# Turned keys written with the page number innermost by VectorE, scores copied as plain rows by ScalarE

## The chip, the cores and the metric

The kernel runs on one core of a Trainium2 chip. Its engines are TensorE (PE), VectorE (DVE), ScalarE (ACT), GpSimd (POOL) and SyncE (SP), which here issues the loads. The metric is the device time of one execution in microseconds (us). Three runs of the kernel before took 1157.41, 1162.14 and 1161.44 us; their median is 1161.44 us.

## The reference

One step of a one-layer decoder trunk with two groups of tokens: a prompt of 512 tokens, and 8 samples (batches) of 8 new tokens each. The layer projects its normalised input to q, k, v and two convolution branches, runs block-sparse attention (8 heads of 64) and a convolution module side by side, projects their concatenation, and ends with a gated convolutional feed-forward network:

```python
h = _rmsnorm(x, g_pre_mix)
z = h @ w_in + b_in
q, k, v, cva, cvg = jnp.split(z, ...)
attn = moba_fn(q, k, v)
...
x = x + _rmsnorm(jnp.concatenate([attn, c], axis=-1) @ w_out, g_post_mix)
...
f = (jax.nn.silu(gate) * val) @ w_down
x = x + _rmsnorm(f, g_post_ffn)
```

The change lies in the attention of the samples. Each sample has 32 cached pages of 128 keys and values, found through a page table; a block is two pages. A query scores the mean key of each of 16 blocks, keeps the best three, and attends to the keys of these and to its own new ones:

```python
kp = pool_k[page_table[:, :npb * ppb]]
k_means = jnp.mean(kp.reshape(DB, npb, MOBA_BLOCK, H, D), axis=2)
idx, slot_ok = _select_blocks(qh, k_means, npb, k_sel)
...
out = _attend(qh, k_s, v_s, sel_mask, k_own, v_own, own_mask)
```

The kernel scores all 4096 cached keys, takes block sums and maxima from the scores, and masks the blocks that were not chosen.

## The kernel before

**Stages.** First x is normalised and turned, and q and the samples' k and v are projected (to about 70 us). Then follow eight sample steps, one for each sample b (about 81 to 503 us). Into them PE's other work is interleaved: steps 0 to 3 each compute a tile of the gated convolution input (`glu_tiles`), steps 4 to 7 a tile of the prompt's k and v (`kv_tiles`). Meanwhile POOL runs three of the four tiles of the 31-tap convolution, and VectorE a part of the fourth (`taps`, in steps 4 to 6). After that come the prompt's attention, the output projection and the feed-forward network (about 505 us to the end), which the change does not touch.

**One sample step.** A sample's 32 pages come in eight groups u of four pages; a page is 256 KB for keys and as much for values. SyncE loads group u of the keys into slot u % 4 of `kN` (128 keys on the partitions, page i, 512 columns of heads), as four transfers. VectorE's `turn_k` then turns 32x32 blocks of a whole group into `kT`, with one STREAM_TRANSPOSE of 2048 elements per partition; there are 8 such instructions a sample, 64 in all. PE multiplies two groups at once with the spread queries (`scores`, j = 0 to 3), into a PSUM bank of 512 columns: group, head half, and 128 columns of that group, in the order that `kT` has them. ScalarE copies the bank to `S` (`put_scores`, 32 copies in all). There the 128 columns are in the order (k i): key number k outer, page number i of four inner. `softmax` on VectorE reduces pairs of pages with that order, and `weigh` on PE picks page i of the turned probabilities.

**What sets the order.** Every engine works through its own list, written by hand, with semaphores between them. VectorE's list for step b is: `softmax(b)`, then `turn_k(b + 1, 0)` and `(b + 1, 1)`, `row_sums(b)` (L1285), `turn_k` of groups 2 and 3, the glu values (steps 0 to 3) or ten taps (steps 4 to 6), `turn_k` of groups 4 to 7, and `norm_out(b)`. Groups 4 to 7 of sample 0 are turned before the loop, groups 0 to 3 of it between the q tiles. PE's list puts `scores(b + 1, (0, 1))` between the first and second half of the values of b, and `scores(b + 1, (2, 3))` at the next step's start, after the output of b has been normalised and turned.

**Loads.** All key and value loads go through SyncE's one list (L313 keys, L323 values), in the order: values 0 to 3 of sample b, keys 0 to 5 of b + 1, values 4 to 7 of b, keys 6 and 7 of b + 1. A transfer waits until its slot is free, and with it all that stand behind it: keys of group u + 4 wait for `turn_k` of group u (`kt_ready`), and values of group u + 4 wait until `weigh` has used group u (`pv_done`), which comes after `row_sums`.

Of the kernel before, what the change touches and what calls it, by code (L numbers as in the profile page):

```python
# [22 lines left out]
ACT = mybir.ActivationFunctionType  # L23
# [67 lines left out]
def build_layer(nc, a):  # L91
    ctx = ExitStack()
    with ctx:
        def sem(name):
            return ctx.enter_context(nc.semaphore(name))
# [26 lines left out]
        def at(mem, off, *dims):  # L122
            n = 1
            for d in dims:
                n *= d
            v = mem[:, off:off + n]
            if len(dims) == 2:
                return v.rearrange("p (a b) -> p a b", a=dims[0])
            if len(dims) == 3:
                return v.rearrange("p (a b c) -> p a b c", a=dims[0], b=dims[1])  # L130
            if len(dims) == 4:
                return v.rearrange("p (a b c d) -> p a b c d", a=dims[0], b=dims[1], c=dims[2])
            return v
# [27 lines left out]
        kT = at(B, 8192, 4, 2 * H, P)  # L161
        vN = at(B, 16384, 4, 4, DA)
        wz = at(B, 24576, KC, 2, P)
        S = at(B, 26624, SUPER, 2, P)
# [85 lines left out]
        SC = [banks["sc0"], banks["sc1"]]  # L250
# [29 lines left out]
        s = {n: sem(n) for n in names}  # L280
# [562 lines left out]
        def _(act):  # L843
# [47 lines left out]
            def put_scores(b, js):  # L891
                if js[0] == 0:
                    act.wait_ge(s["p_turned"], b * 4 + START)
                for j in js:
                    act.wait_ge(s["scores_done"], b * 4 + (j + 1))
                    act.activation(S[:, 2 * j:2 * j + 2].rearrange("p a g (k i) -> p (a g) i k", i=4),  # L896
                                   SC[j % 2][:, :].rearrange("p (c i k) -> p c i k", c=4, i=4), ACT.Copy).then_inc(s["s_put"], 1)

            def exps(b):
                for g in range(2):  # L900
# [49 lines left out]

            act.wait_ge(s["vs_done"], 1)
            put_scores(0, (0, 1))
            with act.Fori(0, 4) as i:
                put_scores(i, (2, 3))
                glu_exps(i)
                exps(i)
                put_turned(i)
                spread_q(i + 1)
                put_scores(i + 1, (0, 1))
                put_out(i)  # L960
# [216 lines left out]
        def _(dve):  # L1177
# [19 lines left out]
            def turn_k(b, u, first=False):  # L1197
                dve.wait_ge(kn_full[u % 4], b * 128 + 64 * (u // 4 + 1))
                if u % 2 == 0 and not first:

                    dve.wait_ge(s["scores_done"], b * 4 + max(u // 2 - 1, 0))
                dve.transpose(kT[:, u % 4, :, :].rearrange("p c (i k) -> p i c k", i=4),  # L1202
                              kN[:, u % 4, :, :].rearrange("p i (c k) -> p i c k", k=32)).then_inc(s["kt_ready"], 1)


# [1 line left out]
            for hp in range(HP):  # L1207
                dve.wait_ge(s["zq_done"], 2 * hp + 2)
                for e in range(2):
                    dve.tensor_scalar(qZ[64 * e:64 * e + 64, hp, e, HALF:TP_], Z[1][64 * e:64 * e + 64, 0:TP_ - HALF],  # L1210
                                      b_in[64 * e:64 * e + 64, hp:hp + 1], None, ALU.add)
                dve.tensor_scalar(qTs[:, hp, :], Z[1][:, TP_ - HALF:HALF], b_in[:, hp:hp + 1], None,
                                  ALU.add).then_inc(s["zq_putV"], 1)
                turn_k(0, hp, True)
# [98 lines left out]
            def step(b, last=False, between=None):  # L1313
                softmax(b)
                if not last:
                    turn_k(b + 1, 0)
                    turn_k(b + 1, 1)
                row_sums(b)
                if not last:
                    turn_k(b + 1, 2)  # L1320
                    turn_k(b + 1, 3)
                if between:
                    between()
                if not last:
                    for u in range(4, 8):
                        turn_k(b + 1, u)
                norm_out(b)
# [373 lines left out]
```

## Time and profile before

| what | value |
|---|---|
| median of three runs | 1161.44 us |
| the profiled execution's own time | 1158.29 us |
| its span in the trace | 1156.5 us |
| mean granted TensorE clock | 0.914 of full speed |
| busy: PE, DVE, ACT, POOL | 970.9, 650.9, 372.0, 584.5 us |
| turning keys on VectorE (L1202) | 64 instructions, 144.7 us busy |
| copies of scores on ScalarE (L896) | 32 instructions, 36.5 us busy |
| start of the sample steps 0 to 7 | 81, 131, 187, 241, 299, 357, 415, 469 us |

The busy times are shares of the whole span, over stages with different limits; the change touches only the stretch up to about 500 us. The start of a sample step is the first block reduction (L1243) of its softmax. PE and PEld overlap, and a busy PE is not a PE at its peak.

### The profile page before, as it was taken

What the parts mean: (1) busy time and instruction counts of PE and PEld (TensorE: products, weight loads), DVE (VectorE), ACT (ScalarE), POOL (GpSimd) and SP (SyncE); (2) the same over time, 40 slices, a digit from 0 to 9 for tenths busy, and PEclk for the clock granted to TensorE, in tenths of its full rate; (3) what the DMA queues carried; (4) which work ended last, traced back from release to release, by engine and by line L of the source; (5) the groups of instructions that cost most, each with busy time, mean ns of one, the idle gap of its engine ahead of it and who ended that gap; (6) DMA issues with size and microseconds to landing.
All of it is one profiled execution on the core that took longest, in us unless ns stands there. A gap on an engine that the chain in (4) does not pass through costs nothing.

```text
span 1156.5 us, 21529 instructions
## 1 busy us (share of the span) xinstructions
PE 970.9 (84%) x7656; PEld 742.5 (64%) x7656; DVE 650.9 (56%) x1009; ACT 372.0 (32%) x683; POOL 584.5 (51%) x534
## 2 busy tenths in 40 slices
PE   4988676776767676778899989999999997999995
PEld 3856464545343534355464449999999997777773
DVE  3478595867798988625712335545554557423114
ACT  3123131313130313234432224433443442134223
POOL 2002999999999994003301115565555563133443
PEclk9999696979787778899899998999999999999998
DMA  9787999999989899971043002223322320222232
GB/s 319 279 277 256 318 319 317 335 323 308 322 287 324 289 317 335 313 239 43 1 164 102 8 1 73 74 73 90 91 73 73 105 77 1 91 73 73 73 87 82
DMA packets 150949, 202.40 MB, mean 175 GB/s; under 512 B 9985, under 2 KB 71426, under 8 KB 150864
## 3 DMA queue, kind: packets, MB, share of 16 engines
q1 hardware_dynamic: 149078, 197.68, 52.4%
q10 hardware_dynamic: 1828, 4.17, 1.1%
q8 instruction: 24, 0.39, 0.1%
q14 instruction: 19, 0.16, 0.0%
HBM read 196.49 MB, written 5.68 MB: 175 GB/s over the span
## 4 chain that ended last, share of the span: by engine, by line
PE 61%; SPq 14%; DVE 9%; issue 6%; DMA 5%; ACT 3%; ACTq 1%; POOL 0%; POOLq 0%; DVEq 0%
SPq L323 10%; PE tp L765 6%; PE z L765 6%; PE sc L765 6%; PE z L812 5%; PE z L741 4%; DMA B<-in_cache_k 3%; PE ob L765 3%; PE sm L765 3%; PE z L470 3%; PE sc L812 3%; PE tp L812 3%; PE sc L741 2%; SPq L313 2%; PE sc L504 2%
## 5 line engine op out<-in xcount | busy, mean ns | idle before, releaser
L1560 POOL TENSOR_SCALAR A<-A,consts 128x512 f32<-128x512 f32 x93 | 150.5, 1618 | 110.9 <-DVE A L1308 101.8
L1202 DVE STREAM_TRANSPOSE B<-B 128x2048 f32<-128x2048 f32 x64 | 144.7, 2291 | 48.1 <-DMA B<-in_cache_k 46.9
L1581 POOL TENSOR_TENSOR wulo<-B,wuhi 128x2048 fp32r<-128x2048 f32 x22 | 108.6, 4938 | 91.5 <-ACT wuhi L1070 64.5
L1563 POOL TENSOR_TENSOR A<-A 128x576 f32<-128x576 f32 x90 | 128.9, 1432 | 7.5
L556 PE MATMUL ob<-B 128*32 128x128 f32 x2048 | 81.9, 321 | 45.2 <-DMA B<-in_cache_v 44.2
L1624 POOL TENSOR_TENSOR wdlo<-B,wdhi 128x1024 fp32r<-128x1024 f32 x22 | 60.0, 2730 | 97.9 <-ACT wdhi L1137 97.9
L556 PEld LDWEIGHTS ob<-B 128*32 128x32 f32 x2048 | 67.7, 147 | 58.5 <-DMA B<-in_cache_v 55.1
L1453 DVE TENSOR_TENSOR fTlo<-A,fThi 128x1152 fp32r<-128x1152 f32 x22 | 32.0, 1455 | 105.6 <-ACT fThi L1136 101.4
L1465 DVE TENSOR_SCALAR B<-B,small 128x512 f32<-128x512 f32 x44 | 25.3, 575 | 115.9 <-ACT B L1108 115.9
L504 PE MATMUL sc<-B,A 128*32 128x256 f32 x1024 | 73.6, 449 | 4.5 <-DVE B L1202 3.9
L1468 DVE SCALAR_TENSOR_TENSOR B<-B,small 128x512 f32<-128x512 f32 x88 | 66.2, 752 | 3.1
L576 PE MATMUL z<-hT,B 128*128 128x288 f32 x256 | 63.1, 408 | 0.0
L504 PEld LDWEIGHTS sc<-B,A 128*32 128x32 f32 x1024 | 37.0, 129 | 37.4 <-issue 23.7
L896 ACT ACTIVATE B<-sc 128x512 f32<-128x512 f32 x32 | 36.5, 1141 | 76.1 <-PE sc L504 76.1
L1611 POOL COPY A<-B 128x2 f32 (+1 forms) x44 | 13.3, 302 | 94.1 <-ACT B L1108 94.1
L1136 ACT ACTIVATE fThi<-A 128x1152 fp32r (+1 forms) x22 | 25.6, 1166 | 103.8 <-PE tp L812 43.9
L576 PEld LDWEIGHTS z<-hT,B 128*128 128x128 f32 x256 | 48.3, 190 | 13.4
L765 PE MATMUL tp<-h2hi,wuhi 128*128 128x288 f32 x176 | 53.4, 303 | 2.2 <-POOL h2lo L1591 2.2
L765 PE MATMUL tp<-h2lo,wuhi 128*128 128x288 f32 x176 | 53.1, 302 | 0.0
L765 PE MATMUL tp<-h2hi,wulo 128*128 128x288 f32 x176 | 53.1, 302 | 0.0
L765 PE MATMUL z<-h2hi,wuhi 128*128 128x288 f32 x176 | 52.2, 296 | 0.0
L765 PE MATMUL sc<-h2lo,wuhi 128*128 128x288 f32 x176 | 52.0, 295 | 0.0
(317 smaller groups left out, 2558.0 us busy)
## 6 DMA issues: line engine op xcount, KB each, us to landing
B<-in_cache_k SPq DMA_DIRECT2D x256, 256.0 KB, 4.8
B<-in_cache_v SPq DMA_DIRECT2D x256, 256.0 KB, 3.9
B<-in_w_up SPq DMA_DIRECT2D x44, 512.0 KB, 4.9
B<-in_w_down SPq DMA_DIRECT2D x22, 512.0 KB, 3.7
B<-in_w_in SPq DMA_DIRECT2D x16, 512.0 KB, 7.2
B<-in_w_in SPq DMA_DIRECT2D x3, 2048.0 KB, 16.7
B<-in_w_out SPq DMA_DIRECT2D x1, 4096.0 KB, 13.9
B<-in_x_prompt SPq DMA_DIRECT2D x4, 512.0 KB, 8.9
```

The source lines that it names most:

```text
L323: sp.dma_start(home[i:P:4, v % 4, :, :], cv[bass.ds(numbers[4 * (v - u) + i], 1)].rearrange("a (g r) n -> (a r) g n", g=4)).then_inc(full[ ...
L504: ins = pe.matmul(SC[j % 2][32 * h4:32 * h4 + 32, :] .rearrange("p (a g k) -> p a g k", a=2, g=2)[:, :, g, :], qS[:, hc, :], kT[:, 2 * (j ...
L556: ins = pe.matmul(OB[32 * hp:32 * hp + 32, 0:P], w, home[:, u % 4, i, hp * P:(hp + 1) * P], start=False, stop=(u == SUPER - 1 and i == 3))
L576: ins = pe.matmul(Z[half][:, 0:HALF], wz[:, k, u, :], hT[:, k, half * HALF:(half + 1) * HALF], start=(k == 0), stop=(k == KC - 1))
L741: ins = pe.matmul(sb_[2 * (t % 2) + nh][0:m, :], mixT[:, k, t * P:t * P + m], wo[:, k, nh * TP_:(nh + 1) * TP_], start=(k == 0), stop=(k = ...
L765: ins = pe.matmul(bank8[4 * slot + n][:, 0:HALF], w[:, u * P:(u + 1) * P], x[:, k, half * HALF:(half + 1) * HALF], start=(k == 0 and j == ...
L812: ins = pe.matmul(db[nh][t][0:m, :], x[:, slot, k2, t * P:t * P + m], w[:, slot, k2, :], start=(first and k2 == 0 and j == 0), stop=(last ...
L1202: dve.transpose(kT[:, u % 4, :, :].rearrange("p c (i k) -> p i c k", i=4), kN[:, u % 4, :, :].rearrange("p i (c k) -> p i c k", k=32)).the ...
L1468: dve.scalar_tensor_tensor(dst[:, 0:TP_], src[:, j:j + TP_], w[:, j:j + 1], dst[:, 0:TP_], ALU.mult, ALU.add)
L1560: pool.tensor_scalar(dst[:, 0:TP_], glu[:, i, j:j + TP_], w, b2, *bias)
L1563: ins = pool.tensor_tensor(conv[:, i, :], conv[:, i, :], prod, ALU.add)
L1581: pool.tensor_tensor(wulo[:, slot, :, :], wu[slot].rearrange("p k u n -> p k (u n)"), wuhi[slot][:, :, :].bitcast(F32), ALU.subtract).then ...
```

## The change

Two access patterns change; no instruction is added, removed or moved on any engine, and the shapes stay (128x2048 for the turning, 128x512 for the copy). VectorE now writes `kT` with page i innermost: the 32 elements of a turned row land 4 elements (16 bytes) apart, where they lay side by side before. PE's result therefore already has the order (k i), and ScalarE's copy writes 512 elements side by side, where it wrote them 16 bytes apart before. `S` holds the same values at the same places as before.

```diff
@@ put_scores, ScalarE
-                    act.activation(S[:, 2 * j:2 * j + 2].rearrange("p a g (k i) -> p (a g) i k", i=4),
-                                   SC[j % 2][:, :].rearrange("p (c i k) -> p c i k", c=4, i=4), ACT.Copy).then_inc(s["s_put"], 1)
+                    act.activation(S[:, 2 * j:2 * j + 2].rearrange("p a g k -> p (a g k)"), SC[j % 2][:, :], ACT.Copy).then_inc(s["s_put"], 1)
@@ turn_k, VectorE
-                dve.transpose(kT[:, u % 4, :, :].rearrange("p c (i k) -> p i c k", i=4),
+                dve.transpose(kT[:, u % 4, :, :].rearrange("p c (k i) -> p i c k", i=4),
                               kN[:, u % 4, :, :].rearrange("p i (c k) -> p i c k", k=32)).then_inc(s["kt_ready"], 1)
```

## Rows read from the trace of the kernel before

**Rows 1.** Busy time in sample steps 0, 1, 4, 5, 6; PEclk, DMA share, GB/s last.
```profile
80.94:131.02 50.08, 34.98 (x478) 26.85 (x478) 35.94 (x49) 12.46 (x24) 21.03 (x20) 0.84 0.85 280
131.02:186.90 55.88, 39.84 (x511) 29.70 (x511) 41.47 (x49) 14.51 (x26) 53.05 (x47) 0.81 0.95 318
...
298.83:357.20 58.37, 39.19 (x483) 24.07 (x475) 51.84 (x64) 13.91 (x24) 55.54 (x48) 0.79 0.92 301
357.20:415.02 57.82, 40.09 (x484) 24.81 (x484) 52.01 (x63) 14.06 (x25) 55.01 (x48) 0.77 0.91 307
415.02:469.21 54.19, 37.52 (x483) 22.55 (x483) 44.28 (x64) 13.90 (x25) 29.85 (x25) 0.81 0.98 329
```

**Rows 2.** Instruction groups: the turning of keys, and what ended VectorE's idle before it.
```profile
L1202 DVE STREAM_TRANSPOSE B<-B 128x2048 f32<-128x2048 f32 x64 | 144.7, 2291 | 48.1 <-DMA B<-in_cache_k 46.9
...
  DMA B<-in_cache_k: 46.9, 13
```

**Rows 3.** Instruction groups: ScalarE's copies, written apart (L896, L884) and side by side.
```profile
L896 ACT ACTIVATE B<-sc 128x512 f32<-128x512 f32 x32 | 36.5, 1141 | 76.1 <-PE sc L504 76.1
...
L913 ACT ACTIVATE B<-tp 128x512 f32<-128x512 f32 x32 | 17.7, 593 | 12.7 <-PE tp L527 12.7
...
L884 ACT ACTIVATE A<-A 32x128 f32 x28 | 12.6, 448 | 0.2
...
L921 ACT ACTIVATE A<-tp 128x128 f32 x7 | 1.9, 277 | 140.1 <-PE tp L564 140.1
```

**Rows 4.** Instruction groups: VectorE's smallest turning, 32 elements.
```profile
L1248 DVE STREAM_TRANSPOSE small<-small 128x32 f32<-128x32 f32 x16 | 3.4, 212 | 0.6
```

**Rows 5.** VectorE in time, sample step 1: start, duration, instruction, idle before and releaser.
```profile
138.14 0.69 DVE L1243 TENSOR_REDUCE small<-B 128x8 f32<-128x512 f32 x1 [0.39 <-ACT B L896]
...
152.28 4.49 DVE L1202 STREAM_TRANSPOSE B<-B 128x2048 f32<-128x2048 f32 x2
156.69 1.05 DVE L1285 TENSOR_TENSOR small<-small 128x2 f32<-128x2 f32 x1
157.67 4.49 DVE L1202 STREAM_TRANSPOSE B<-B 128x2048 f32<-128x2048 f32 x2
162.54 3.75 DVE L1298 RECIPROCAL A<-A 128x576 f32<-128x576 f32 x1
...
167.55 4.50 DVE L1202 STREAM_TRANSPOSE B<-B 128x2048 f32<-128x2048 f32 x2
181.20 2.31 DVE L1202 STREAM_TRANSPOSE B<-B 128x2048 f32<-128x2048 f32 x1 [9.15 <-DMA B<-in_cache_k]
184.10 2.31 DVE L1202 STREAM_TRANSPOSE B<-B 128x2048 f32<-128x2048 f32 x1 [0.59 <-DMA B<-in_cache_k]
186.34 0.13 DVE L1289 RECIPROCAL small<-ob 128x1 f32<-128x1 f32 x1
```

**Rows 6.** SyncE's list and PE's first values in time, sample step 1.
```profile
141.76 17.08 SPq L313 DMA_DIRECT2D B<-in_cache_k  x24
160.45 13.23 SPq L323 DMA_DIRECT2D B<-in_cache_v  x16
174.59 4.21 SPq L313 DMA_DIRECT2D B<-in_cache_k  x8
...
158.61 5.34 PE L556 MATMUL ob<-B 128*32 128x128 f32 x128
```

**Rows 7.** VectorE in time, ahead of the sample steps and in step 0.
```profile
39.71 0.92 DVE L1210 TENSOR_SCALAR A<-z,consts 64x224 f32<-64x224 f32 x2 [4.25 <-PE z L470]
...
70.16 0.68 DVE L1230 TENSOR_TENSOR A<-tp,A 64x512 f32<-64x512 f32 x1 [4.88 <-PE tp L490]
72.13 8.89 DVE L1202 STREAM_TRANSPOSE B<-B 128x2048 f32<-128x2048 f32 x4 [1.28 <-PE sc L504]
...
125.56 2.31 DVE L1202 STREAM_TRANSPOSE B<-B 128x2048 f32<-128x2048 f32 x1 [12.48 <-DMA B<-in_cache_k]
```

## The prediction

> **What bounds the kernel now.** I read the busy times over the sample steps first, then the groups of instructions for what the two edited lines cost, and last the timelines of VectorE and of SyncE's list through one step.
>
> The busy times show two kinds of step. In step 1 the DMA engines are busy 0.95 of the time and VectorE 41.47 of 55.88 us; in steps 4 and 5 VectorE is busy 51.84 of 58.37 and 52.01 of 57.82 us, and the DMA share is 0.92 and 0.91 [rows 1]. So steps 0 to 3 go at the pace of the loads, with some room on VectorE, and steps 4 to 6, where VectorE has the ten taps as well, are close to full on it. The room has a place and a size: over all 64 turnings VectorE waits 13 times for a key load, 46.9 us in sum [rows 2]. In step 1 the reader sees it as 9.15 us ahead of group 6 and 0.59 ahead of group 7, the last but two things VectorE does in the step [rows 5]; step 0 has 12.48 us at the same place [rows 7]. Steps 2 and 3 repeat step 1.
>
> What ends a step is therefore group 7 of the next sample's keys: after it VectorE normalises the output, PE turns that and computes the next scores, and the next softmax follows. Before it stands a loop through the loads. Keys 4 and 5 wait for the turning of groups 0 and 1, values 4 to 7 stand behind them and wait for the values of the step, which wait for the row sums, and keys 6 and 7 come after those [rows 5, 6].
>
> **ScalarE's copies.** A copy of 512 columns written 16 bytes apart takes 1141 ns; the copy of the same size from PSUM written side by side takes 593 ns [rows 3]. I take 593 for the new one: 548 ns less for each of 32, 17.5 us of ScalarE in all. On the path lies little of it. Copies 0 and 1 of a sample are made while VectorE turns keys, far ahead. Copies 2 and 3 lie between the scores at the step's start and the reductions, which wait for them (0.39 us ahead of the last pair) [rows 5]; but the copy of j = 2 runs while PE computes j = 3, so a step gains one 0.55 us, 8 times: 4.4 us.
>
> **VectorE's turning.** No row shows VectorE writing single words 16 bytes apart, so the price is bounded. The one end is nothing: 2291 ns as now [rows 2]. For the other, ScalarE's rows show exactly this write pattern. From 128 columns in 277 ns and 512 in 593 follow 0.82 ns a column and 172 ns fixed when the words lie side by side; written apart, 1141 ns is (1141 - 172) / 512 = 1.89 ns a column, 1.07 more [rows 3]. If memory sets the rate and it is the same for VectorE, a turning with a fixed part of 179 ns (from 212 ns for 32 elements and 2291 for 2048, 1.03 ns an element) [rows 2, 4] takes 179 + 2048 x 1.89 = 4.05 us, 1.76 more. If the addition per word is the same, it takes 2291 + 2048 x 1.07 = 4.48 us, 2.19 more. The other copy written 16 bytes apart takes 448 ns for 128 columns against 277, 1.34 ns a column more [rows 3], which would be 2.74 us on a turning; that copy is short and covers 32 partitions, so I keep it as the far end. I take 2.0 us, between the two readings of the nearest row: a turning of 4.3 us, eight of them 34 us in a step instead of 18.
>
> The Trainium skill speaks against this change: the page Vector Engine (DVE) Microarchitecture Reference, section 5.2 Measured stream behaviour on trn2, says that a port of VectorE keeps its rate only while words come in adjacent pairs, and gives 1.71 ns a column for a destination that hops every element by 4 KiB and about 2.5 for steps of 24 words. No row here shows VectorE doing so. An estimate from that page's figures is 1.4 to 3.0 us more for a turning, and by the same sum as below a time of 1206 to 1286 us.
>
> **Where the turnings lie.** The first four, between the q tiles, are hidden: VectorE waits 4.25 us for PE after such a turning [rows 7], more than 2.0; behind the fourth the copies of q end later, but PE is busy with the values' projection until 70.13 us, as the wait of 4.88 us shows [rows 7]. Groups 4 to 7 of sample 0 run back to back for 8.89 us ahead of the first softmax [rows 7], on the path: 4 times. The other 56 stand in steps 0 to 6, in order with everything else of VectorE. So 60 x 2.0 = 120 us are added to VectorE's line.
>
> Against that stands the cover of 46.9 us. It is not free, since the loop of the loads moves too. In step 1 the turn of group 6 comes after six slower turnings, 12 us later. Its keys also land later: values 4 to 7 are let go by the values of the step, which wait for the row sums, and these come after two slower turnings, 4 us later (they were released at 156.69 + 1.05 us, and SyncE went on at 160.45) [rows 5, 6]. Of the wait of 9.15 us, 8 are used and about 1 us is left; the same in steps 2 and 3. In step 0 I reckon the loads 2 us later, so 10 of 12.48 are used. So about 4 us of waiting stays, and 43 are used up. In steps 4 to 6 the taps already fill the time, there are 5.8 us of waits among them, and the turnings cost nearly their whole 16 us a step.
>
> Who else waits: PE's scores of groups 0 and 1, 2 and 3 and the values behind them come 4 to 8 us later in the step, but have until its end. SyncE's keys 6 and 7 wait for groups 2 and 3, which are turned long before the values ahead of them are issued. After step 7 nothing is changed.
>
> **Sum.** 120 (60 turnings) - 46.9 (waits) + 4 (waits that stay) - 4.4 (copies) = 72.7 us. Against the profiled execution's 1158.3 us that is 1231 us. That execution lies 3.2 us below the median of 1161.4, and I leave it there.
>
> **The rivals.**
> 1. The waits do not give way. If late slots starve the loads so that half of the 46.9 us stays, the sum is 96 us and the time about 1254; if all of it stays, 116 us and 1274. For it: the DMA share is 0.95 in step 1, and each load stands behind a wait on VectorE [rows 1, 6]. Against it: a longer step needs no more bytes; step 1 moves 318 GB/s x 55.9 us = 17.8 MB, and over 63 us that is 283 GB/s, so the loads then have room.
> 2. VectorE writes apart at its full rate. Then only the copies count, 0.55 us a step: 1158.3 - 4.4 = 1154 us at best, no change where the loads take it up again. The place is the write side of the turning, and it decides the sign: below about 0.1 us more for a turning the kernel is no slower. For it: a turning now runs at 1.03 ns an element, as fast as any stream of VectorE in these rows [rows 2, 4], so the block is read and written at once without loss. Against it: ScalarE loses 1.07 ns a column on the same addresses [rows 3]. The same page of the Trainium skill, section 3.8 The reshape front-end and per-opcode configuration, says that the transposing block is pipelined to sustain one element per cycle and lane; if that held for any destination it would be this rival.
> 3. The price is small, 0.5 to 0.8 us, so that steps 0 to 3 hide most: 60 x 0.65 = 39, less what hides there (32 x 0.65 = 21) and 4.4, makes some 14 us and 1172. No row speaks for such a price.
>
> **How the numbers follow.** Forecast 0.73: with 1.76 us a turning 106 - 46.9 + 10 - 4.4 = 65 us, 1223; with 2.19 us 131 - 46.9 + 2 - 4.4 = 82 us, 1240; with 2.74 us 164 - 46.9 - 4.4 = 113 us, 1271. Rival 1: 0.16. Rival 2: 0.07. Rival 3: 0.04. The range from 1203 to 1274 us holds the forecast with 20 us below its lower price, and rival 1 up to its end; the rest, rivals 2 and 3 and a little above, is below 2 in 10. A difference of 0.5% (5.8 us) is about what a measurement of this kernel can tell from no change. Slower by more than that: 0.92 (forecast, rivals 1 and 3). Within: 0.05, and faster by more: 0.03, both from rival 2, whose 4.4 us lie inside the bound.
>
> **What would show it.** L1202 in the groups of the profile after: about 4.3 us if right, 2.3 if rival 2 is. L896: about 0.6 us. VectorE's waits for key loads: a few us instead of 46.9; 20 or more would be rival 1. Step 1 about 63 us long, step 4 some 73, and the stretch from the prompt's attention to the end as long as before. The prediction is wrong if the turning keeps its time, or if the steps grow by far more or less than 60 turnings less the waits.

## The result and the profile after

The changed kernel takes 1204.61 us (median of 4 runs, 1201.82 to 1206.04) against 1161.79 us of the kernel before in the same comparison: a ratio of 1.0371, 95% interval 1.0335 to 1.0407. It is slower by 43 us. The profiled executions differ by the same: 1201.82 us against 1158.29 us.

The groups of instructions of the changed kernel hold the two edited lines (the turning is L1201 now). Columns: busy time, mean ns of one, idle before with what ended it.

```profile
L1201 DVE STREAM_TRANSPOSE B<-B 128x2048 f32<-128x2048 f32 x64 | 243.9, 3907 | 12.3 <-DMA B<-in_cache_k 11.0 <-PE sc L504 1.3
...
L896 ACT ACTIVATE B<-sc 128x512 f32<-128x512 f32 x32 | 19.1, 598 | 105.6 <-PE sc L504 105.6
```

A turning takes 3907 ns where it took 2291 [rows 2]: 1616 ns more, 64 times. The copy takes 598 ns where it took 1141 [rows 3]. And the cover, the waits for key loads in which longer turnings can hide, is mostly gone: VectorE waits 11.0 us, not 46.9 [rows 2]. Each half of the change has an effect, but they are of very different weight, since a turning writes 2048 words a partition and a copy 512, and the one stands on VectorE's line and the other mostly beside it.

The busy times over the sample steps of the changed kernel (columns as in [rows 1]; PE, PEld, DVE, ACT, POOL, then PEclk, DMA share, GB/s) show where the time went. The last row is everything after the start of step 7.

```profile
86.69:140.49 53.80, 35.93 (x478) 26.77 (x478) 48.62 (x50) 10.26 (x23) 17.36 (x17) 0.82 0.72 242
140.49:198.70 58.21, 38.53 (x511) 28.01 (x511) 51.03 (x48) 12.38 (x26) 55.33 (x48) 0.82 0.93 307
...
319.22:385.63 66.41, 36.51 (x475) 21.73 (x467) 62.01 (x65) 11.39 (x24) 63.11 (x55) 0.78 0.91 302
385.63:455.10 69.47, 37.93 (x484) 22.36 (x484) 63.42 (x64) 11.70 (x25) 66.11 (x57) 0.77 0.78 261
455.10:512.58 57.48, 36.75 (x483) 22.14 (x483) 52.19 (x64) 11.67 (x25) 4.01 (x4) 0.80 0.81 268
...
512.58:1200.00 687.42, 638.67 (x3844) 511.43 (x3844) 305.74 (x565) 252.36 (x462) 257.69 (x243) 0.97 0.27 82
```

Step 1 grew by 2.3 us, step 4 by 8.0, step 5 by 11.7, step 6 by 3.3 [rows 1]. In step 5 the DMA share fell from 0.91 to 0.78 and in step 6 from 0.98 to 0.81, as the loads there now wait for VectorE: SyncE's list waits 15.8 and 13.4 us for turnings in these two steps, where it waited 2.3 and nothing. The stretch from step 7 to the end is 687.4 us, as it was (1156.5 - 469.2 = 687.3). All of the 43 us lies between 72 us and the start of step 7.

VectorE's timeline in step 1 of the changed kernel answers to [rows 5]: two slow turnings, the row sums, two more, the glu values, and then the last four, with a wait of 2.80 us where 9.15 and 0.59 stood.

```profile
158.74 7.80 DVE L1201 STREAM_TRANSPOSE B<-B 128x2048 f32<-128x2048 f32 x2
166.39 0.15 DVE L1284 TENSOR_TENSOR small<-small 128x2 f32<-128x2 f32 x1
166.42 8.04 DVE L1201 STREAM_TRANSPOSE B<-B 128x2048 f32<-128x2048 f32 x2
...
180.37 7.61 DVE L1201 STREAM_TRANSPOSE B<-B 128x2048 f32<-128x2048 f32 x2
190.78 7.47 DVE L1201 STREAM_TRANSPOSE B<-B 128x2048 f32<-128x2048 f32 x2 [2.80 <-DMA B<-in_cache_k]
```

One row in it was not expected: the row sums (L1284, before L1285) take 0.15 us where they took 1.05 [rows 5].

**The account of VectorE's line.** From the first of the four turnings ahead of the loop to the start of step 7 the kernel before needs 397.1 us (72.13 to 469.21), the changed one 440.6 us (72.02 to 512.58), 43.5 more. VectorE's busy time in that stretch rises from 316.3 to 398.9 us, of which the 60 turnings take 135.5 and 228.4: +92.9 us for the turnings, -10.4 us for all its other instructions. Its waits for key loads fall by 35.9 us, and those for the copies from 20.7 to 17.2 us, by 3.5. The sum, 92.9 - 10.4 - 35.9 - 3.5, is 43.1 us. (60 x 1.616 would be 97.0 us; in the records turnings that follow one another overlap a little, as four in a row take 14.67 us and not 15.6.)

The rows of this account, first the two stretches before and after, then the turnings and the waits for copies in them:

```profile
72.13:469.21 397.08, 276.18 (x3524) 187.58 (x3516) 316.29 (x388) 102.15 (x180) 320.85 (x276) 0.81 0.93 311
72.02:512.58 440.56, 273.40 (x3524) 183.89 (x3516) 398.87 (x388) 85.43 (x180) 320.48 (x276) 0.79 0.86 285
...
L1202 DVE STREAM_TRANSPOSE B<-B 128x2048 f32<-128x2048 f32 x60 | 135.5, 2290 | 48.1 <-DMA B<-in_cache_k 46.9 <-PE sc L504 1.3
L1201 DVE STREAM_TRANSPOSE B<-B 128x2048 f32<-128x2048 f32 x60 | 228.4, 3910 | 12.3 <-DMA B<-in_cache_k 11.0 <-PE sc L504 1.3
...
DVE small L1243 <- ACT B L896: 20.7, 12, 3.0
DVE small L1242 <- ACT B L896: 17.2, 13, 2.5
```

TensorE's granted clock in this stretch is 0.79 of full speed after and 0.81 before. That is no term of the sum: besides the waits for copies, VectorE waits for PE 1.3 us in both kernels.

### The profile page after: what moved, and what is told of

It reads as the page before. It is cut to its first block, busy times and chain, and to the rows that moved or that the text cites. A ratio compares the mean times of both kernels' runs of the same rounds, so it can differ in the third digit from the quotient of the medians.

```text
span 1200.0 us, 21529 instructions
## 1 busy us (share of the span) xinstructions
PE 968.3 (81%) x7656; PEld 738.0 (62%) x7656; DVE 740.9 (62%) x1009; ACT 354.5 (30%) x683; POOL 584.7 (49%) x534
## 4 chain that ended last, share of the span: by engine, by line
PE 59%; DVE 20%; issue 8%; SPq 6%; DMA 3%; ACT 2%; DVEq 1%; ACTq 0%; POOL 0%; POOLq 0%
DVE B L1201 10%; PE tp L765 6%; PE z L765 6%; PE sc L765 6%; PE z L812 5%; SPq L323 4%; PE z L741 3%; PE sc L504 3%; PE ob L765 3%; PE sm L765 3%; PE sc L812 3%; PE z L470 3%; PE tp L812 3%; PE sc L741 2%; DMA B<-in_cache_k 2%
## 5 line engine op out<-in xcount | busy, mean ns | idle before, releaser
L1201 DVE STREAM_TRANSPOSE B<-B 128x2048 f32<-128x2048 f32 x64 | 243.9, 3907 | 12.3 <-DMA B<-in_cache_k 11.0
L504 PE MATMUL sc<-B,A 128*32 128x256 f32 x1024 | 76.0, 456 | 17.2 <-DVE B L1201 16.6
L564 PE MATMUL tp<-consts,oN 128*128 128x128 f32 x8 | 3.6, 456 | 89.2 <-DVE oN L1291 89.2
L1570 POOL TENSOR_TENSOR A<-A,B 128x2304 f32<-128x2304 f32 x1 | 5.0, 5047 | 110.9 <-ACT B L1032 110.9
L576 PEld LDWEIGHTS z<-hT,B 128*128 128x128 f32 x256 | 48.3, 190 | 13.4
```

The lines of the kernel that those rows point to most:

```text
L504: ins = pe.matmul(SC[j % 2][32 * h4:32 * h4 + 32, :] .rearrange("p (a g k) -> p a g k", a=2, g=2)[:, :, g, :], qS[:, hc, :], kT[:, 2 * (j ...
L576: ins = pe.matmul(Z[half][:, 0:HALF], wz[:, k, u, :], hT[:, k, half * HALF:(half + 1) * HALF], start=(k == 0), stop=(k == KC - 1))
L1201: dve.transpose(kT[:, u % 4, :, :].rearrange("p c (k i) -> p i c k", i=4), kN[:, u % 4, :, :].rearrange("p i (c k) -> p i c k", k=32)).the ...
```

## The experiments

The diffs are shortened: `...` marks what is left out, `S[...]` and `SC[...]` stand for whole indices, and `kT[:, u % 4]` stands for `kT[:, u % 4, :, :]`. Where a kernel writes the turned keys or the scores in another order than the softmax expects, its results are not the reference's, but its instructions and their shapes are those of the kernel that it is compared with.

**The halves apart, and VectorE's time alone.** The first kernel takes only ScalarE's half.

```diff
-  S[:, 2*j:2*j+2].rearrange("p a g (k i) -> p (a g) i k", i=4), SC[j % 2].rearrange("p (c i k) -> p c i k", c=4, i=4)
+  S[:, 2*j:2*j+2].rearrange("p a g k -> p (a g k)"), SC[j % 2][:, :]
```

> Only ScalarE's half of the change: plain copies, turned keys side by side as before. The columns of the scores then stand in the order (i k), which the softmax takes for (k i), so keys are put to the wrong blocks; every instruction keeps its shape. Theory (VectorE's line sets the steps): copies 0.6 us, turnings 2.29 us, 0.55 us less a step, about 1157 us. Rival (the loads take the gain up in the load-bound steps 0 to 3): 1159 to 1161 us.

Measured: 1154.77 us, ratio 0.9939 (0.9921 to 0.9958) to 1161.85 us before. The copies take 597 ns, the turnings 2288. The theory was close (7 us less, 4.4 expected); the rival, that the loads take the gain up, is out, since even the upper end of the interval is 4.9 us below the time before.

The second takes only VectorE's half.

```diff
-  dve.transpose(kT[:, u % 4].rearrange("p c (i k) -> p i c k", i=4), ...)
+  dve.transpose(kT[:, u % 4].rearrange("p c (k i) -> p i c k", i=4), ...)
```

> Only VectorE's half: keys turned with the page innermost, ScalarE's copies written apart as before (so the scores are permuted once too often; shapes as before). Theory: turnings 3.9 us, and the gain of the copies gone: the changed kernel's 1204.6 us and 3.5 to 4.4 us more, about 1208 us. Rival (the copies are hidden behind the longer turnings): 1205 us as the changed kernel.

Measured: 1205.05 us, ratio 1.0374 (1.0352 to 1.0395); turnings 3910 ns, copies 1131. The group of its turning:

```profile
L1202 DVE STREAM_TRANSPOSE B<-B 128x2048 f32<-128x2048 f32 x64 | 243.8, 3910 | 12.6 <-DMA B<-in_cache_k 11.3 <-PE sc L504 1.3
```

The slow-down is in the turning alone. What the copies bring once the turnings are slow stays open: the time equals that of the full change, as the rival has it, but VectorE's waits for the copies are 21.7 us here against 17.2 with the full change, as the theory has it, and 3 to 4 us is not more than the runs of either kernel scatter.

The third kernel leaves all addresses as before and only gives VectorE more to do.

```diff
+  dve.tensor_reduce(fill[...], kN[:, u % 4].rearrange("p i n -> p (i n)")[:, 0:1408], AX.X, ALU.max)
   dve.transpose(kT[:, u % 4].rearrange("p c (i k) -> p i c k", i=4), ...)
```

> The kernel before, with a reduction of 1408 key columns (about 1.62 us, read side by side, result not used) put ahead of each of the 64 turnings on VectorE, and nothing written apart by VectorE. Theory (it is only VectorE's time): 2.29 + 1.62 = 3.91 us for each turning with its filler, so the same time as the turning-alone kernel within 3 us, about 1208 us. Rival (words written 16 bytes apart also slow others: loads into the same memory, PE's reads of the turned keys): the filler kernel is faster than the turning-alone kernel by 5 us or more.

Measured: 1207.75 us, ratio 1.040 (1.038 to 1.042). The groups of this kernel, the filler and the turning:

```profile
L1206 DVE STREAM_TRANSPOSE B<-B 128x2048 f32<-128x2048 f32 x64 | 147.0, 2297 | 0.0
L1204 DVE TENSOR_REDUCE fill<-B 128x1408 f32 x56 | 89.0, 1590 | 13.6 <-DMA B<-in_cache_k 13.6
```

1590 and 2297 ns make 3.89 us, nearly the slow turning's 3.91, and the time is 2.7 us above the turning-alone kernel, with the waits down to 13.6 us in the same way. (The filler's group above has 56 of its 64 instructions; the other 8 take 1598 ns.) So 1.6 us more on VectorE ahead of each key group is enough for the whole effect, and no sign is left of words written apart slowing anyone else: PE's scores take 456 ns a matmul in the changed kernel and 459 in this one.

**Where ScalarE may pay instead.** The permutation can also be put into the copy's reads: ScalarE reads PSUM 32 words apart and writes side by side.

```diff
-  S[...].rearrange("p a g (k i) -> p (a g) i k", i=4), SC[...].rearrange("p (c i k) -> p c i k", c=4, i=4)
+  S[...].rearrange("p a g (k i) -> p (a g) k i", i=4), SC[...].rearrange("p (c i k) -> p c k i", c=4, i=4)
```

> The kernel before with ScalarE's copy in the other order: it reads PSUM 32 words apart and writes side by side; turnings as before, all values at the same places. If reading PSUM apart is free: copies 0.6 us and the time of the copy-alone kernel, about 1157 us, better than both kernels. If it costs what writing apart costs: copies 1.1 us and 1161 us, as before.

Measured: 1153.77 us, ratio 0.994 (0.9923 to 0.9956), with every value of `S` where it was before. It is faster than both kernels. The line of its copy:

```profile
L896 ACT ACTIVATE B<-sc 128x512 f32<-128x512 f32 x32 | 19.1, 598 | 81.2 <-PE sc L504 81.2
```

598 ns is the plain copy's time: reading PSUM 128 bytes apart costs ScalarE nothing here, where writing 16 bytes apart cost it 543 ns.

**What it is about the addresses.** Two kernels write the turned rows in other patterns, with the same instructions and the changed kernel's plain copies. Both still read the keys word by word in the old order, so only the writes differ. First pairs of neighbouring words, a step of 8 words from pair to pair:

```diff
-  kT[:, u % 4].rearrange("p c (k i) -> p i c k", i=4)
+  kT[:, u % 4].rearrange("p c (m i z) -> p i c m z", i=4, z=2)
```

> As the changed kernel, but the turning writes its rows in pairs: two neighbouring words, then a step of 8 words (positions (16 pairs of keys, page, 2)). The order of keys and pages in the columns is then not the one the softmax expects; shapes and counts are as before. Theory (a line is paid for each single word apart): pairs are free, turnings 2.3 us, the time of the copy-alone kernel, about 1155 us. Rival (any row that isn't side by side pays): turnings 3.9 us and about 1205 us.

Measured: turnings 2288 ns; 1155.26 us, ratio 0.9965 (0.9937 to 0.9993). Pairs are free.

Then single words 2 words apart:

```diff
-  kT[:, u % 4].rearrange("p c (k i) -> p i c k", i=4)
+  kT[:, u % 4].rearrange("p c n -> p (c n)").rearrange("p (h k y) -> p y h k", y=2, k=32)
```

> As the changed kernel, but single words are written 2 words (8 bytes) apart; the order of the columns isn't the one the softmax expects. If two words that fall into the same 16 bytes one after the other are enough for the full rate: turnings 2.3 us, about 1155 us. If the words must be neighbours: turnings 3.5 to 4.2 us, about 1205 us.

Measured: turnings 2295 ns; 1154.98 us, ratio 0.9966 (0.9942 to 0.9991). Neighbours are not needed: in all the patterns tried, the turning keeps its rate where two words one after the other fall into the same 16 bytes, and loses it where each falls into 16 bytes of its own. Steps of 3 words, and pairs that lie across a boundary of 16 bytes, were not tried, so the exact limit stays open. The group of the turning in this run:

```profile
L1201 DVE STREAM_TRANSPOSE B<-B 128x2048 f32<-128x2048 f32 x64 | 144.9, 2295 | 46.2 <-DMA B<-in_cache_k 44.5 <-PE sc L504 1.6
```

Last, larger steps: 16 words and 64 words.

```diff
+  kT[:, u % 4].rearrange("p c n -> p (c n)").rearrange("p (i k c) -> p i c k", i=4, c=16)    # 16 words
+  kT[:, u % 4].rearrange("p c n -> p (c n)").rearrange("p (k i c) -> p i c k", i=4, c=16)    # 64 words
```

> As the changed kernel, but single words are written 16 words (64 bytes) apart, order of the columns not kept. If only single words apart matter: 3.9 us a turning as with 4 words, about 1205 us. If small steps cost more than large ones or the reverse: between 3.5 and 5.5 us, and 60 times the difference in the time (5.0 us would give about 1265 us, since nearly no wait for loads is left as cover).

> As the changed kernel, but single words are written 64 words (256 bytes) apart, order of the columns not kept. The same expectation as for 16 words: 3.9 us a turning and about 1205 us if the step's size does not matter; 3.5 us and about 1185 us if large steps are cheaper.

Measured: 16 words 3663 ns a turning and 1194.56 us; 64 words 3752 ns and 1202.19 us, one run of each. The group of the first:

```profile
L1201 DVE STREAM_TRANSPOSE B<-B 128x2048 f32<-128x2048 f32 x64 | 228.6, 3663 | 19.8 <-DMA B<-in_cache_k 18.5 <-PE sc L504 1.3
```

The step's size matters little once each word is alone in its 16 bytes: 3.66 to 3.91 us. The larger steps are a little cheaper than 4 words; no step near 5 us came.

**GpSimd's part.** The account above has 10.4 us that came back on VectorE's other instructions. GpSimd runs its convolution beside them, and the timelines show how the two meet. In the kernel before, in step 1, GpSimd's addition that is under way as the row sums start (156.69 us, 1.05 us long [rows 5]):

```profile
156.33 1.40 POOL L1563 TENSOR_TENSOR A<-A 128x576 f32<-128x576 f32 x1
```

The row sums end at 157.74, as GpSimd's addition does at 157.73. The same stands in steps 1 to 6: the addition starts 0.34 to 0.38 us ahead of the row sums, which take 1.04 to 1.08 us. In the changed kernel both start together, and the row sums take 0.15 us:

```profile
166.39 0.15 DVE L1284 TENSOR_TENSOR small<-small 128x2 f32<-128x2 f32 x1
166.39 1.44 POOL L1562 TENSOR_TENSOR A<-A 128x576 f32<-128x576 f32 x1
```

In its steps 1 to 5 the row sums start at the same time as the addition or up to 0.15 us ahead of it, and take 0.14 to 0.15 us. So two slower turnings move the row sums to another point of GpSimd's cycle. The filler kernel, which has the same shift and writes nothing apart, has 0.12 us there as well. The row sums alone are 5.5 of the 10.4 us. The end of GpSimd's convolution counts too: its work is the same, the steps are longer, and so it is busy for only 4.0 us of step 6, where it was busy for 29.9 [rows 1]; VectorE's other work in that step falls by 4.1 us (row sums included). To size GpSimd's part, both kernels were run with nearly nothing on GpSimd.

```diff
-                for j in range(CW):
+                for j in range(2):
...
```

> The kernel before with 2 of the 31 convolution taps on GpSimd (29 of 31 taps of three tiles left out), so that GpSimd is nearly idle during the sample steps. Theory (VectorE's short two-input instructions wait for GpSimd's): the row sums take 0.15 us in every step instead of 1.05, VectorE's other work in steps 0 to 6 shrinks by 10 to 20 us, some of it turned into waits for loads: 1145 to 1155 us.

> The changed kernel with the same 29 of 31 taps left out on GpSimd. Theory: VectorE sets every step, so what it no longer waits for GpSimd comes off in full; nothing is won back by a lucky phase against GpSimd, so the difference to the quiet kernel before is larger than the 43 us of the full pair by up to 10 us: 45 to 55 us, about 1200 us. Rival (GpSimd plays no part in the difference): 43 us again.

Measured: 1148.75 us before (ratio to the full kernel before 0.9894, 0.9864 to 0.9924), 1174.31 us after (1.0112, 1.008 to 1.0143). The first time came as expected, the second did not: the change costs 26 us with a quiet GpSimd, less than the 43 with a busy one. The waits of VectorE say why; columns: who waited for whom, total us, times, longest. Quiet before:

```profile
DVE B L1202 <- DMA B<-in_cache_k: 71.0, 31, 11.7
```

Quiet after:

```profile
DVE B L1201 <- DMA B<-in_cache_k: 13.3, 4, 3.7
```

VectorE's other work from the first of the four turnings ahead of the loop to step 7 is 276.7 - 136.9 = 139.8 us before (73.90 to 456.46 us) and 366.0 - 227.7 = 138.3 us after (71.47 to 484.05 us), where the busy pair had 180.8 and 170.4. So a quiet GpSimd does take away the 10 us that came back (1.5 are left), as the theory says, but it takes 41 us off VectorE's other work in the kernel before and 32 in the changed one, where 10 to 20 were expected for the first. In the kernel before 24 us of that turn into waits for loads, 71.0 us instead of 46.9, and the change can hide 57.7 us behind them instead of 35.9. The account closes here too: turnings +90.8, waits for loads -57.7, other work -1.5 and waits for copies -1.6 (21.5 to 19.9) make 30.0 us, and the stretch grows by 412.6 - 382.6 = 30.0 us. (The profiled executions differ by 27.9 us, since the four turnings begin 2.4 us earlier in the second.) The expectation had GpSimd's piece right and left out that a large part of what VectorE saves in the kernel before turns into waits for loads, which are new cover for the slower turnings.

## Why the prediction was right, and where its terms were off

The forecast was slower by 73 us, 1231 us in a range of 1203 to 1274; measured are 1204.6 us, 1.6 us above the range's lower end. The direction, the place and the mechanism came as written: the turnings cost more, 60 of them lie on the path, the waits for key loads are used up, and nothing after step 7 moves. The filler kernel shows that mechanism by itself. The size was off: step 1 took 58.2 us and step 4 66.4, where 63 and 73 were forecast. That the time still lies in the range is owed to the 20 us that were left below the forecast's lower price, and is in part luck. Rival 2 (VectorE writes apart at its full rate) and rival 1 (the waits do not give way) are out by one row, 3907 ns with 11.0 us of waits; rival 3 by the price. (Rival 1's case of half the waits counts the 4 us that stay twice: 120 - 23.5 - 4.4 is 92 us and 1250, not 96 and 1254.) Three terms were mis-sized, two of them making the forecast too long and one too short:

- **The price of a turning**, 2.0 us, measures 1.616, and 60 of them 92.9 us on VectorE's line, not 120. The nearer reading of ScalarE's row was that of an equal rate: (3907 - 179) / 2048 is 1.82 ns an element, against ScalarE's 1.89. Taking the middle between "same rate" and "same addition" cost 60 x 0.38 = 23 us, most of the miss. The Trainium skill, Vector Engine (DVE) Microarchitecture Reference, section 5.2 Measured stream behaviour on trn2, gives 1.71 ns a column for a destination that hops by 4 KiB at every element. The runs show 1.70 for 16 words and 1.74 for 64, close to it, though none of them hops as far. The same section of the Trainium skill gives 2.5 ns for steps of 24 words, a step that no run here has. The adjacent pairs that this section of the Trainium skill asks for are more than these runs need: single words 2 words apart ran at the full rate (2295 ns). The Trainium skill, SBUF — State Buffer, section Door 1: The DMA port swizzle, says that SBUF has lines of 16 bytes and needs at least two hits on a line for full bandwidth; the kernel with 2 words (2295 ns) and the one with 4 (3907 ns) agree with that.
- **The cover**: 43 us were to be used up, and 35.9 were; 11.0 us stay, not 4. With a smaller price less of the wait is reached, as the lower case of the forecast had it. The loop of the loads came as the prediction drew it: six slower turnings less the two that hold the loads back are four prices, 6.5 us at the measured price, and steps 1 to 3 lose 6.9, 6.6 and 6.6 us of their waits.
- **VectorE's other work** was left at nothing and gave back 10.4 us, since the row sums and other short instructions met GpSimd's work at other points, and since GpSimd had nearly finished when step 6 came. That term was missing. It is a part of why steps 4 and 6 did not cost "nearly their whole" price of the turnings: these add 12.3, 12.4 and 12.0 us in steps 4 to 6, which grew by 8.0, 11.7 and 3.3. In step 6, 4.4 us of waits for loads are used up and 4.1 us of other work fall away.

The copies' 4.4 us were about right: 7 us in the copy-alone kernel and 4.5 and 4.8 in the pairs and two-word kernels, which have plain copies and full-rate turnings too, and 3.5 us of waits in the changed kernel. With the measured terms the sum of the prediction is 92.9 - 35.9 - 3.5 - 10.4 = 43 us.

The paragraph on who else waits was right too: the loads were not starved. Step 5 moves at 261 GB/s instead of 307, and the DMA engines have room there.

## What to carry to other kernels

When a permutation has to be paid, try the side that reads PSUM: here the same reordering cost 543 ns on a copy of 512 words as ScalarE's writes, 1616 ns on a turning of 2048 words as VectorE's writes, and nothing as ScalarE's reads from PSUM. Before giving an engine more work, read its waits in the stage as a store of cover, count how much of it the longer work reaches (35.9 of 46.9 us here), and ask what else fills the same store. When a float32 turning on VectorE has to write an inner dimension apart, try an order in which two words one after the other fall within 16 bytes; for ScalarE's writes only a step of 16 bytes was tried.

## What the runs showed of the hardware that was not expected

VectorE's turning wrote single words 8 bytes apart at the full rate (2295 ns for 2048 elements), 16 bytes apart at 3907, 64 at 3663 and 256 at 3752. ScalarE read PSUM 128 bytes apart without loss (598 ns against 593 to 598 for plain reads). A VectorE addition of 2 columns took 1.05 us when it started inside a GpSimd addition, and ended with it, and 0.15 us when both started at once; with the order of the work fixed, the same meeting came back in each of steps 1 to 6.
